# The triangular inverse of a chunked recurrence: from rows inside 16x16 blocks to products from 2x2 blocks up

## What is computed

```python
def step(state, inp):
    r_t, w_t, k_t, v_t, a_t, b_t = inp
    sa = jnp.einsum('bhvk,bhk->bhv', state, a_t)
    state = (state * w_t[:, :, None, :] + sa[..., None] * b_t[:, :, None, :]
             + v_t[..., None] * k_t[:, :, None, :])
    return state, jnp.einsum('bhvk,bhk->bhv', state, r_t)

_, out = lax.scan(step, s0, xs, reverse=reverse)
```

## Time and profile before

| | |
|---|---|
| median of 3 executions | 3286.42 us |
| span of the profiled execution (first to last instruction) | 3290.5 us |
| stretch in which the recurrence runs | about 535 to 1310 us of the span |
| TensorE (PE) busy in the whole span | 3119.3 us (95%) |
| VectorE (DVE) busy in the whole span | 2068.6 us (63%) |
| ScalarE (ACT), GpSimd (POOL) busy | 1069.2 us (32%), 366.4 us (11%) |
| mean granted TensorE clock | 0.976 of full speed |

### The profile page before, as it was taken

One profiled execution on the slowest core, in us unless ns is written; L12 is line 12 of the kernel. 1 busy time (PEld: TensorE's weight loads), 2 busy tenths in 40 slices (PEclk: granted clock), 3 DMA queues, 4 the chain that ended last, 5 costly groups with the idle time before them and its releaser, 6 DMA issues.

```text
span 3290.5 us, 51924 instructions
## 1 busy us (share of the span) xinstructions
PE 3119.3 (95%) x21878; PEld 2507.8 (76%) x21878; DVE 2068.6 (63%) x3255; ACT 1069.2 (32%) x1528; POOL 366.4 (11%) x338
## 2 busy tenths in 40 slices
PE   8998997788988888999999999999999999999999
PEld 7787885676767676778888888887746888788887
DVE  6665554477677775645544444468979988755444
ACT  5222334444444442222111111132244332433332
POOL 0322441000000000401000000020000000110000
PEclk9999999899899998999999999999999999999999
DMA  3333666234344324421111111111101222223222
GB/s 148 131 130 106 227 206 180 68 90 100 75 107 101 96 60 145 156 88 52 52 52 52 39 52 52 52 39 44 47 13 52 90 103 103 88 92 120 98 91 76
DMA packets 93527, 301.85 MB, mean 92 GB/s; under 512 B 10352, under 2 KB 38640, under 8 KB 70768
## 3 DMA queue, kind: packets, MB, share of 16 engines
q1 hardware_dynamic: 79104, 246.63, 24.2%
q0 software_dynamic: 14192, 51.91, 4.6%
HBM read 241.35 MB, written 57.15 MB: 91 GB/s over the span
## 4 chain that ended last, share of the span: by engine, by line
PE 55%; DVE 5%; DMA 1%; ACT 1%; issue 1%; POOL 0%; SPq 0%; DVEq 0%; POOLq 0%; ACTq 0%
PE ps L2444 24%; PE ps L308 21%; PE ps L2250 2%; PE ps L2606 2%; DVE Yh L2633 2%; PE ps L2066 1%; DVE wlo L288 1%; DMA gl<-gts 1%; PE ps L330 1%; PE ps L2527 1%; PE ps L2768 0%; PE ps L2483 0%; PE ps L2708 0%; DVE xT L2812 0%; DVE rsh L2513 0%
## 5 line engine op out<-in xcount | busy, mean ns | idle before, releaser
L2444 PE MATMUL ps<-Hh,whi 128*128 128x512 f32 x1600 | 497.9, 392 | 1.3 <-DVE uA L2565 0.7
L284 ACT ACTIVATE whi<-raw 128x2048 fp32r<-128x2048 f32 x139 | 265.5, 1910 | 522.3 <-PE ps L308 296.5
L288 DVE TENSOR_TENSOR wlo<-raw,whi 128x2048 fp32r<-128x2048 f32 x139 | 321.1, 2310 | 95.1 <-ACT whi L284 94.8
L2444 PEld LDWEIGHTS ps<-Hh,whi 128*128 128x128 f32 x1600 | 300.0, 188 | 70.6 <-issue 5.3
L2444 PE MATMUL ps<-Hh,wlo 128*128 128x512 f32 x800 | 311.3, 389 | 0.0
L308 PE MATMUL ps<-Hhi,wlo 128*128 128x512 f32 x672 | 206.9, 389 | 0.0
L308 PE MATMUL ps<-Hhi,whi 128*128 128x512 f32 x672 | 206.9, 389 | 0.0
L308 PE MATMUL ps<-Hlo,whi 128*128 128x512 f32 x672 | 206.8, 389 | 0.0
L2444 PE MATMUL ps<-aHh,whi 128*128 128x512 f32 x512 | 199.5, 390 | 2.7 <-DVE wlo L288 2.5
L2444 PE MATMUL ps<-aLh,whi 128*128 128x512 f32 x512 | 199.2, 389 | 0.0
L2444 PE MATMUL ps<-aHh,wlo 128*128 128x512 f32 x512 | 199.2, 389 | 0.0
(11 more groups left out here) (389 smaller groups left out, 6144.8 us busy)
## 6 DMA issues: line engine op xcount, KB each, us to landing
raw<-in_panels SPq DMA_DIRECT2D x139, 1024.0 KB, 4.8
rwf<-F POOLq DMA_DIRECT2D x16, 1280.0 KB, 6.7
L<-rwf SPq DMA_DIRECT2D x16, 1024.0 KB, 5.0
L<-rwf SPq DMA_DIRECT2D x64, 256.0 KB, 3.9
Dn<-nbs SPq DMA_DIRECT2D x128, 128.0 KB, 5.6
gts<-so POOLq DMA_DIRECT2D x16, 512.0 KB, 3.4
gl<-gts SPq DMA_DIRECT2D x32, 256.0 KB, 3.8
rwt<-so POOLq DMA_DIRECT2D x15, 512.0 KB, 3.0
```

The lines of the kernel that those rows point to most:

```text
L284: e.activation(whi[i % 2][:, :], raw_of(i)[:, :], AF.Copy).then_inc(*a_hi.up(i))
L288: e.tensor_tensor(wlo[i % 2][:, :], raw_of(i)[:, :], whi[i % 2][:, :].bitcast(F32), OP.subtract).then_inc(*v_lo.up(i))
L2444: m = e.matmul(ap, W[wi][:, kc, n0:n0 + 128], mov[mi][:, kc, :], start=x == 0 and q == 0, stop=x == len(kcs) - 1 and q == 2)
```

## The change

The inverse is now built from 2x2 blocks. A strictly triangular 2x2 block has one element a, and the inverse of (I - A) is I + A, so `base` writes XT = (A masked to the 2x2 diagonal blocks) + I in one vector operation. From there five levels double the blocks (2 to 4, 8, 16, 32, 64) with the products of levels 4 and 5 of before. The constant `bm` masks 2x2 blocks instead of 16x16, and the mask of a level is now one value per partition and pair of blocks, broadcast over the block's columns. `Nc`, the DRAM buffer, its transfers, all rows and `spread` are gone. GpSimd clears five Y buffers in a step instead of two. The loads of the gate and bonus of a step (`gate_sp`) move from piece `row3` to piece `X4`. A step has 26 slots instead of 27, and one 0 is taken out of `EACH`. The number of attention pieces is the same.

```diff
-                    ("lmask", 4 * 64), ("bm", 64), ("id16", 16), ...
+                    ("lmask", 2 * 31), ("bm", 64), ...
+LEVELS = (1, 2, 3, 4, 5)
-            x.Dn = sb(f"Dn{d}", kb + 0, [128, 2048])
+            x.Y2 = sb(f"Y2{d}", kb + 6, [128, 8, 64])
+            x.Y3 = sb(f"Y3{d}", kb + 4, [128, 8, 64])
+            x.Ys = {1: E2, 2: x.Y2, 3: x.Y3, 4: x.Y, 5: E3}
 # TensorE
-        if c in ("Y4", "Y5"):
+        if c in INVERSE and c[0] == "Y":
-            if lev == 4:
+            if lev == 1:
                 e.wait_ge(*a.by(s, "X"))
             else:
-                e.wait_ge(*v.by(s, "XT", 4))
+                e.wait_ge(*v.by(s, "XT", lev - 1))
             ap = wtake(e, d, s, ("Y", lev), (v, s, "Y", lev))
             for i, (h, p) in enumerate(HH):
                 for cc_ in range(2):
                     m = e.matmul(ap[cols(cc_), 32 * i:32 * (i + 1)], x.SC[cols(cc_), p, BA, h, :],
                                  part(x.X[cols(cc_), i, :], lev, d), start=True, stop=True)
-        if c in ("X4", "X5"):
+        if c in INVERSE and c[0] == "X":
             ...
 # VectorE
-        if c == "Nc":
+        if c == "base":
             e.wait_ge(*v.by(s, "bm"))
             if s:
-                e.wait_ge(*d_n[d].by(s - 1, "st"))
-            e.tensor_reduce(x.Nc[:, :, :], ..., AX, OP.add)
-            e.tensor_tensor(x.Nc[:, :, :], x.Nc[:, :, :], id16, OP.add)
-            e.tensor_copy(x.Xc[:, :, :], id16)
-        if c in ROWS_OF:
-            for n in ROWS_OF[c]:
-                e.tensor_tensor(x.pr[:, :, 0:n + 1], x.Xc[:, :, u], Dv[:, :, u, y], OP.mult)
-                e.tensor_reduce(x.Xc[:, :, y:y + 1], x.pr[:, :, 0:n + 1], AX, OP.add)
-        if c == "spread":
-            e.wait_ge(*v.by(s, "row", 15))
-            if s:
                 e.wait_ge(*t.by(s - 1, "WU", 1))
-            e.tensor_tensor(x.XT[:, :, :], x.Xc (broadcast), K("bm", 64) (broadcast), OP.mult)
+            e.tensor_tensor(x.XT[:, :, :], x.E1[:, :].rearrange("p (h c) -> p h c", h=8),
+                            K("id64", 64)[:, None, :].broadcast_to([128, 8, 64]), OP.add)
 # GpSimd
-        if c == "spread":
-            e.memset(x.Y[:, :, :], 0.0)
-            e.memset(x.Y2[:, :, :], 0.0)
+        if c == "base":
+            e.wait_ge(*v.by(s, "XT0"))
+            for lev in LEVELS:
+                e.memset(x.Ys[lev], 0.0)
 # SyncE
-        if c == "Nc":
-            e.dma_start(nb, x.Nc[:, :, :].rearrange("p h t -> p (h t)"))
-            e.wait_ge(*d_n[d].by(s, "st"))
-            e.wait_ge(*t_w[d].by(s, "SC", 1))
-            for q in range(8):
-                e.dma_start(x.Dn[16 * q:16 * (q + 1), :], ...)
-        if c == "row3":
+        if c == "X4":
             gate_sp(e, d, s)
 # the order
-    BEFORE = ("cum", "mul", "turn", "scores", "PV", "Nc")
-    BETWEEN = ("S0", "S1", "post1", "row0", "row1", "post2", "row2", "post3", "row3", "row4", "row5")
-    AFTER = ("spread", "X", "Y4", "X4", "Y5", "X5", "WU", "RG", "OH")
+    BEFORE = ("cum", "mul", "turn", "scores", "PV", "base")
+    BETWEEN = ("S0", "X", "S1", "Y1", "post1", "X1", "Y2", "post2", "X2", "Y3", "post3", "X3")
+    AFTER = ("Y4", "X4", "Y5", "X5", "WU", "RG", "OH")
-    EACH = (0, 0, 1, 1, 1, 1, 0, 0, 1, 1, 0, 0, 1, 1, 0, 1, 1, 0, 1, 0, 0, 1, 1, 1, 1, 0, 1)
+    EACH = (0, 0, 1, 1, 1, 1, 0, 0, 1, 1, 0, 0, 1, 1, 0, 1, 1, 0, 1, 0, 1, 1, 1, 1, 0, 1)
```

More of the change, by code:

```diff
@@ L73, in constants @@
             c[:, o + 64 * i:o + 64 * (i + 1)] = m
[L74 to L80, removed]
+        for lev in LEVELS:
+            for g in range(32 >> lev):
+                c[:, CC["lmask"] + 31 * d + LMASK[lev] + g] = (r[:, 0] >> lev) == 2 * g + 1 - d
+    c[:, CC["bm"]:CC["bm"] + 64] = (r // 2) == (np.arange(64)[None, :] // 2)
     c[:, CC["bd"]:CC["bd"] + 128] = same
@@ L1217, in build @@
     t_w, v_w, a_w, g_w = ([signals(f"{x}_w{d}") for d in range(2)] for x in "tvag")
-    d_l, d_g, d_n, d_ob = ([landings(f"{x}{d}", n) for d in range(2)] for x, n in (("d_l", 3), ("d_g", 2), ("d_n", 9), ("d_ob", 1)))
+    d_l, d_g, d_ob = ([landings(f"{x}{d}", n) for d in range(2)] for x, n in (("d_l", 3), ("d_g", 2), ("d_ob", 1)))
     d_lng = landings("d_lng", 1)
@@ L1258, in build @@
     KA, KR, BA, BR = range(4)
-    ROWS_OF = {"row0": range(1, 4), "row1": range(4, 7), "row2": range(7, 10), "row3": range(10, 12), "row4": range(12, 14),
-               "row5": range(14, 16)}
+    INVERSE = {f"{a}{lev}": lev for a in "YX" for lev in LEVELS}
     def tile_of(d, s):
@@ L1532, in w_act @@
             e.wait_ge(*v_w[d].by(s, "O-mu"))
-            e.wait_ge(*(v_w[d].by(s + 1, "Nc0") if s < 7 else t.by(s, "H")))
+            e.wait_ge(*(v_w[d].by(s + 1, "XT0") if s < 7 else t.by(s, "H")))
             e.activation(x.E1[:, :], x.Os[:, :], AF.Square).then_inc(*a.up(s, "O2"))
@@ L1608, in w_dve @@
+            e.tensor_tensor(x.XT[:, :, :], x.E1[:, :].rearrange("p (h c) -> p h c", h=8),
+                            K("id64", 64)[:, None, :].broadcast_to([128, 8, 64]), OP.add).then_inc(*v.up(s, "XT0"))
+        if c in INVERSE and c[0] == "Y":
+            lev = INVERSE[c]
+            Y = x.Ys[lev]
+            m = K("lmask", 32 >> lev, 31 * d + LMASK[lev])[:, None, :, None].broadcast_to([128, 8, 32 >> lev, 1 << lev])
             e.wait_ge(*t.by(s, "Y", lev))
             e.wait_ge(*g.by(s, "Y0", lev))
-            e.tensor_tensor(part(Y[:, :, :], lev, d), packed(wring.bank(d, s, ("Y", lev)), lev), m,
+            e.tensor_tensor(part(Y, lev, d), packed(wring.bank(d, s, ("Y", lev)), lev), m,
@@ L1611, in w_dve @@
                             OP.mult).then_inc(*v.up(s, "Y", lev))
-        if c in ("X4", "X5"):
-            lev = int(c[1])
+        if c in INVERSE and c[0] == "X":
+            lev = INVERSE[c]
             if lev < 5:
                 Xs = part(x.X[:, :, :], lev, d)
-                e.wait_ge(*t.by(s, "X4"))
-                e.tensor_tensor(Xs, packed(wring.bank(d, s, "X4"), lev), Xs, OP.add).then_inc(*v.up(s, "X", 4))
+                e.wait_ge(*t.by(s, "X", lev))
+                e.tensor_tensor(Xs, packed(wring.bank(d, s, ("X", lev)), lev), Xs, OP.add).then_inc(*v.up(s, "X", lev))
@@ L1679, in w_pool @@
         x, v, g = D[d], v_w[d], g_w[d]
-        if c == "spread":
-            e.wait_ge(*v.by(s, "row", 15))
-            e.memset(x.Y[:, :, :], 0.0).then_inc(*g.up(s, "Y0", 4))
-            e.memset(x.Y2[:, :, :], 0.0).then_inc(*g.up(s, "Y0", 5))
+        if c == "base":
+            e.wait_ge(*v.by(s, "XT0"))
+            for lev in LEVELS:
+                e.memset(x.Ys[lev], 0.0).then_inc(*g.up(s, "Y0", lev))
         if c == "post2":
@@ L1856, in slots @@
                     made.append((d, *calls[i]))
-            more = FRONT[k] if k < LATER else EACH[(k + 4) % 27] if k < n - AHEAD else 2
+            more = FRONT[k] if k < LATER else EACH[(k + 4) % 26] if k < n - AHEAD else 2
             for _ in range(min(more, UNITS - at)):
```

54 lines of the change are left out of this document (11 added, 43 removed).

## The result

The kernel after takes 3409.3 us (median of 4 runs, 3397.7 to 3423.0) against 3286.6 us before: 1.037 times as long, with a 95% interval of 1.033 to 1.040. The forecast was 3338 us. The direction was right, but the loss is 123 us and not 52. The profiled execution took 3405.73 us, with a span of 3403.9 us.

What follows compares the result with a forecast made beforehand. TensorE, 86% busy in the recurrence, was taken as the bound. 3290.5 + 140 (groups) - 51 (idle) - 37 (clock) = 3342.5 us profiled, 4.1 us over the median, so 3338 us; range 3272 to 3390 us.

Steps and rivals of the forecast that it cites:

- the price of a group: TensorE, levels 1 to 3: 144 new groups of 16 matmuls at 0.97 us each add 140 us.
- Rival 3: Products cost more: level 1's short runs double its groups or instruction supply stalls; 3382 to 3393 us, chance 0.11.
- which idle time goes: TensorE's waits for the read-back, AP, X and RG, and half the issue waits: 71 us go, 36 us stay.
- rival 2: VectorE was the true bound, so its 78 us less work shortens the stretch: 3208 us, chance 0.04.
- what frees a bank is an operation that the hand-overs above already wait for: PSUM's ring of four banks, taken 9 times more in a step: no wait beyond those already counted.
- The idle term: TensorE's idle time in the recurrence: 56 us instead of 107, so minus 51 us.
- No wait over 3 us for VectorE: Sign expected in the profile after: TensorE never waits over 3 us for VectorE.
- the clock: TensorE's low clock in the recurrence: 18 of 55 us lost remain, minus 37 us; granted clock 0.95 or more.
- With idle time halved and the long waits gone I keep a third of the loss: Step of the clock term: less idle time leaves 18 of the 55 us lost to low clock.
- Rival 1: Idle time and clock recover more than 140 of 162 us, 0.87 us a group: 3271 us, chance 0.14.
- Rival 4: It doesn't matter: gains near 140 us keep the time within 0.2%, chance 0.07.
- the signs of a wrong forecast: A period under 91 us, group starts under 0.9 or over 1.2 us apart, or a clock near 0.91.

Runs made afterwards that it cites:

- e1: The kernel after with levels 1 to 3 left out on TensorE and VectorE (inverse wrong): 3238.6 us, 0.986 of before.
- e9: The kernel after with 64 moving columns in its levels and post1 behind X1, level 1 left out (inverse wrong): 3279.4 us, 0.997 of before.
- e6: The kernel after with piece post1 moved behind X1, so X1's vector addition goes ahead of it: 3356.3 us, 1.020 of before.
- e3: The kernel after with 64 instead of 32 moving columns in the matmuls of levels 1 to 3: 3379.4 us, 1.029 of before.
- e5: The kernel after with 64 columns in levels 1 to 3, without these levels' vector operations and waits (inverse wrong): 3300.0 us, 1.003 of before.
- e2: The kernel after with the matmuls of levels 1 to 3 but without their vector operations and waits (inverse wrong): 3316.6 us, 1.010 of before.
- e8: The kernel before with 64 moving columns in levels 4 and 5, nothing else: 3280.4 us, 0.997 of before.
- e11: The kernel before with 64 columns in levels 4 and 5 and the rows one slot later, behind post2: 3277.1 us, 0.997 of before.
- e7: The kernel after with 64 moving columns in all five levels and post1 behind X1: 3318.6 us, 1.009 of before.

## Why the prediction was right and wrong

**Right: the price of a group.** 0.97 us and 140 us were said. 0.93 us and 134 us were measured, between the kernel after and e1 (0.92 by the closer reading). Between before and after the closer reading gives 125 us, or 0.87 us each, and e9's groups of 64 columns cost 0.91 us. Runs of 2, 4 and 8 words instead of 16 cost nothing visible. e9 can't show it, since its wide groups read whole rows; the trace of the kernel after does. Only level 1 makes an `X` (L1395) out of `E`, with runs of 2 words, and that group starts 0.96 us before the next one here (and 0.90 us in the other way, at 1087 us):

```profile
1038.35 1.12 PE L1395 MATMUL ps<-E,XT 64*64 64x32 f32 x32
1039.31 1.10 PE L1401 MATMUL ps<-XT,E 64*64 64x32 f32 x32
```

Rival 3's doubled groups are out, and so are columns as the measure of price.

**Right: which idle time goes.** The read-back, `AP` and `RG` waits vanish. The issue waits of L1415 were to be halved from 10.5 us; after, those of all lines come to 6.8 us. `Y4` was to wait about 2 us for the late addition; the row of L1384 has 2.4 us at most. VectorE was to be 441 us busy and is 434 us; that it isn't the bound is shown by e1, so rival 2 is out.

**Wrong: "what frees a bank is an operation that the hand-overs above already wait for".** This is the step on PSUM's ring. A bank is freed by an operation in VectorE's order, and TensorE asks for it in its own order, long before the product chain would ask for the same addition. The new 3.4 us wait (24.0 us in all) is this, and e6 shows it by taking it away. The idle term was minus 51 us and came out at minus 41 us. Behind the 10 us stands a larger error that others balanced: 24 us of `OH` that weren't foreseen. "No wait over 3 us for VectorE" failed by the same step.

**Wrong, and most of the miss: the clock.** The term was minus 37 us, and it came out at plus 13 us (plus 21 by the closer reading). The step that failed is "With idle time halved and the long waits gone I keep a third of the loss". The loss itself was read well (55 us said, 54 by the closer reading), and an earlier sentence, "The low stretches come after idle time", holds in every trace. But the loss does not shrink with the idle time: idle time fell by 41 us and the waits of 5 us and more went, and there were 24 low stretches instead of 18 and 160 us at 1.2 GHz instead of 130. Between groups of 32 columns waits of 0.5 us were enough, and the change added 144 such groups and a chain with such waits among them. e3 against the kernel after, and e5 against e2, show it by widening these groups and no other edit. I had seen the clock of 0.87 in a period without a long wait and read past it. The sum with all of the loss given back was put at 3319 us; by its own terms (3338 less 18) it is 3320 us.

**The sum.** Forecast for the stretch: 140 - 51 - 37 = plus 52 us. Measured: 134 - 41 + 13 = plus 106 us, against 105.4 us read. Of the 71 us between forecast and median, the clock accounts for 50 (58 by the closer reading) and idle time for 10, less 6 for the groups that were cheaper (15 by the closer reading). 8 us came outside the stretch, where the program is the same: the low clock costs 20 us there in the profiled execution after and 10 us in that of before. With the same code it costs 10 to 21 us there in the experiments, so this part is chance. 9.5 us are how the profiled spans stand to the medians: 4 us above before, 5 us below after.

**The rivals.** Rival 1 wanted idle time and clock to return more than 140 us. In e5, where both are nearly exhausted (28 us and nearly nothing left), they return 137 of the 165 us, against 136 us of work, and the time is 0.3% above before. So even its best case is about a draw in this order of pieces. Its "0.87 us a group" was not far off: the least between two starts shown is 0.90 us, and the closer reading gives 0.87 to 0.92. Rival 4, a draw within 0.2%, is near what e5 gives and not what the change does. Of the signs of a wrong forecast, a clock near 0.91 came true. A period was to take 97 to 101 us; the two shown take 101.09 and 107.36 us, the three around them 105.1, 109.6 and 105.6 us. "TensorE over 90% busy" held, at 791 of 857 us.

**Still open.** Why a wait of 0.5 us is followed by a low stretch among narrow groups and not among wide ones isn't shown, only that it is so in these traces. Nor is it shown why not every such wait is (four of six in e2). The waits of `Y4` (18 us in e7) remain; the one order that I tried against them moved them elsewhere.

## What to carry to other kernels

Where a group of small matmuls costs the same at twice the columns, try it with the wider operand: it cost under 10 us of work here and gave 0.9% (e3), and 0.3% to a kernel that had few such groups (e8). Don't forecast the clock from the sum of idle time; count the short waits between small matmuls as well. When a chain of products is added to an engine that is already the bound, its price is the number of groups times their distance from start to start, and that has to be set against all that idle time and clock can give back (165 us here) before anything else is argued. For each buffer of a shared ring, look up which operation frees it and what stands ahead of that operation in its engine's order; one exchange of two pieces was worth 53 us.

## What the runs showed of the hardware

In all thirteen traces TensorE's granted clock fell, within the recurrence, only shortly behind an idle time. With groups of 32 moving columns in 64x64 tiles, waits of 0.5 us were enough (the kernel after at 1054 us, e2 behind four of its six waits of 0.5 us); where the groups of the levels had been widened to 64 the shortest wait ahead of a fall was 1.4 us (e8, e11). With 64 columns the clock of the stretch came out higher at some 5 us of difference in idle time or less: 0.91 to 0.95 with the chain, 0.96 to 1.00 without it. I had taken the amount of idle time as the only cause.

A group of 32 records of such matmuls (16 matmuls, two records each) has nearly the same distance from start to start at 32 as at 64 columns, 0.90 and 0.94 us, while one with 128 columns takes 1.89 us. Runs of 2 words in the moving operand don't lengthen it (0.90 and 0.96 us in the kernel after).
